# Routing weights of half the tokens: from one-hot matrix products to adding indirect DMAs and a GpSimd multiply

## The reference, cut to what matters

```
q = (ht @ w_q).reshape(T, PEER_HEADS, 2, PEER_HALF)
scores = einsum('thcd,hckd->thck', q, sub_keys)
s1, i1 = top_k(scores[:, :, 0], 16);  s2, i2 = top_k(scores[:, :, 1], 16)
cand_s = s1[..., :, None] + s2[..., None, :]          # 256 candidates a head
cand_i = i1[..., :, None] * 128 + i2[..., None, :]
top_s, pos = top_k(cand_s, 16);  idx = take_along_axis(cand_i, pos);  g = softmax(top_s)
act = gelu(einsum('pd,phkd->phk', hb, u[idx]))
out = einsum('phk,phkd->pd', g * act, v[idx])
```

## Time and profile before

| | |
|---|---|
| median of 3 runs | 2611.45 us |
| profiled execution, first to last instruction | 2611.0 us |
| busy PE, DVE, ACT, POOL | 2444.0, 1762.2, 1563.5, 28.8 us |
| mean granted clock of PE | 0.992 of full |
| moved by DMA | 413.64 MB, 158 GB/s |

### The profile page before, as it was taken

The page is one execution under the profiler, slowest core; times in us unless marked ns, Lnnn a source line. Parts: engine busy times, 40 slices in busy tenths (PEclk is TensorE's granted clock), DMA queues, the critical chain, the costliest instruction groups (busy, mean ns, idle before and its releaser), DMA issues.

```text
span 2611.0 us, 54286 instructions
## 1 busy us (share of the span) xinstructions
PE 2444.0 (94%) x16994; PEld 2251.7 (86%) x16994; DVE 1762.2 (67%) x4132; ACT 1563.5 (60%) x3546; POOL 28.8 (1%) x96
## 2 busy tenths in 40 slices
PE   8898989999999679999999989999999996899998
PEld 7798888999999568888899978899999995688887
DVE  4557775687774986666656667647777659766666
ACT  4476755555554875555556677456555558655555
POOL 0000100000000000000000001000000000000000
PEclk9999999999999999999999999999999999999999
DMA  5454445455555005555544543454555540255554
GB/s 186 168 174 137 146 146 176 148 187 181 178 176 181 12 33 194 192 192 194 192 168 163 171 132 121 162 177 161 178 187 181 177 145 0 81 193 193 193 193 169
DMA packets 116277, 413.64 MB, mean 158 GB/s; under 512 B 7860, under 2 KB 18028, under 8 KB 115948
## 3 DMA queue, kind: packets, MB, share of 16 engines
q1 hardware_dynamic: 116204, 412.73, 46.6%
HBM read 411.09 MB, written 4.23 MB: 159 GB/s over the span
## 4 chain that ended last, share of the span: by engine, by line
PE 80%; DVE 10%; ACT 4%; issue 3%; DMA 2%; DVEq 1%; ACTq 0%; POOL 0%; SPq 0%; POOLq 0%
PE bank L281 16%; PE bank L282 16%; PE bank L283 16%; PE bank L296 9%; PE bank L298 9%; PE bank L297 9%; DVE hot L1403 3%; DMA raw<-stream 2%; DVE w_lo L263 2%; DVE hot L1407 1%; ACT w_hi L250 1%; DVE A L1413 1%; PE bank L373 1%; ACT L323 1%; PE bank L1031 1%
## 5 line engine op out<-in xcount | busy, mean ns | idle before, releaser
L263 DVE TENSOR_TENSOR w_lo<-raw,w_hi 128x512 fp32r<-128x512 f32 x1512 | 1026.9, 689 | 772.1 <-ACT w_hi L250 761.0
L250 ACT ACTIVATE w_hi<-raw 128x512 fp32r<-128x512 f32 x1512 | 904.6, 626 | 390.2 <-PE bank L298 313.3
L281 PE MATMUL bank<-h_hi,w_hi 128*128 128x256 f32 x3488 | 999.5, 287 | 28.9 <-DVE w_lo L263 27.4
L282 PE MATMUL bank<-h_lo,w_hi 128*128 128x256 f32 x3488 | 989.0, 284 | 0.0
L283 PE MATMUL bank<-h_hi,w_lo 128*128 128x256 f32 x3488 | 988.7, 283 | 0.0
L281 PEld LDWEIGHTS bank<-h_hi,w_hi 128*128 128x128 f32 x3488 | 671.1, 192 | 39.9 <-DVE w_lo L263 31.8
L282 PEld LDWEIGHTS bank<-h_lo,w_hi 128*128 128x128 f32 x3488 | 671.3, 192 | 0.4
L283 PEld LDWEIGHTS bank<-h_hi,w_lo 128*128 128x128 f32 x3488 | 671.2, 192 | 0.0
L296 PE MATMUL bank<-w_hi,a_hi 128*128 128x512 f32 x1088 | 426.6, 392 | 8.3 <-issue 5.0
L297 PE MATMUL bank<-w_lo,a_hi 128*128 128x512 f32 x1088 | 425.9, 391 | 0.0
L298 PE MATMUL bank<-w_hi,a_lo 128*128 128x512 f32 x1088 | 425.3, 391 | 0.0
(11 more groups left out here) (180 smaller groups left out, 1881.8 us busy)
## 6 DMA issues: line engine op xcount, KB each, us to landing
raw<-stream SPq DMA_DIRECT2D x378, 1024.0 KB, 4.8
hank<-rel_hankel SPq DMA_DIRECT2D x16, 256.0 KB, 2.7
rel_hankel<-rel_line SPq DMA_DIRECT2D x8, 384.0 KB
hank<-rel_hankel SPq DMA_DIRECT2D x16, 128.0 KB, 2.2
A<-subkeys SPq DMA_DIRECT2D x2, 1024.0 KB, 4.9
x<-x_in SPq DMA_DIRECT2D x2, 512.0 KB, 3.8
pr<-lru_w SPq DMA_DIRECT2D x2, 512.0 KB, 7.3
out<-x SPq DMA_DIRECT2D x4, 256.0 KB, 2.0
```

The costliest lines, as they stand in the source:

```text
L250: act.activation(w_hi[:, (ring % 2) * 2 + k, :], raw[:, slot, sub, 512 * k:512 * k + 512], ACT.Copy).then_inc(w_hi_done, 1)
L263: dve.tensor_tensor(w_lo[:, q, :], raw[:, slot, sub, 512 * k:512 * k + 512], w_hi[:, q, :].bitcast(F32), ALU.subtract).then_inc(w_parts, 1)
L281: pe.matmul(ps, hi, rhs_hi(4 * k + c), start=first, stop=False)
L282: pe.matmul(ps, hi, rhs_lo(4 * k + c), start=False, stop=False)
```

## The change

Tokens 0 to 127 and tokens 128 to 255 are now treated apart.

- The top-k work is done in two passes over U, each for one half of the tokens (8 heads) and over 56 blocks (`HALF`): lists, candidates, candidate lists, softmax. The transposes stand behind block 116 (`FREE`) instead of 112.
- For tokens 0 to 127, DVE computes after the first pass, around block 53 of U, the address of each pick in a DRAM table `spread_w` (`cell_at` = index x 128 + token), and the weights `mass`. POOL then issues 128 indirect DMAs a layer, one for each head and rank, each of 128 single floats (one a partition, that is a token) that are added to the table in DRAM. Before the first of each head after the first it waits until all those of the heads before have landed.
- The tables (one a layer, 128 x 128 x 128 floats, 8 MB) are cleared by 16 DMAs a layer that POOL issues in the mixer, ahead of its wait for `on_sum`.
- When U is done, POOL fetches the table in 16 parts of 512 KB into four tiles that lie over `h_hi` and `h_lo`, and multiplies each into `A[:, 8i:8i+8, 0:128]`. The first split of V waits for the last of these too.
- The one-hot stage goes over tokens 128 to 255 alone: 32 groups instead of 64.

```diff
-N_GROUPS = SEQ // 4
+N_GROUPS = P // 4
@@ mix_gpsimd, between the last bias tile and the wait for on_sum
+                if layer == 0:
+                    pool.memset(zeros[:], 0.0).then_inc(zeros_set, 1)
+                    pool.wait_ge(zeros_set, 1)
+                for i in range(16):
+                    pool.dma_start(spread_w[layer][8 * i:8 * i + 8].rearrange("e (a b) t -> (e a) (b t)", a=16).rearrange("p (n f) -> p n f", f=512),
+                                   spread(zeros[:].rearrange("p (n f) -> p n f", n=1), 1, 2)).then_inc(cleared.sem, 16)
@@ the retrieval
-            FREE = 112
+            FREE = 116
+            HALF = 56
-            UNITS = TT * PEER_HEADS
+            UNITS = PEER_HEADS
+            def peer_gpsimd(pool, layer):
+
+                cells = spread_w[layer].rearrange("a b (t o) -> (a b t) o", o=1)
+                pool.wait_ge(cleared.sem, cleared.base)
+                pool.wait_ge(mass_done.sem, mass_done.base + 1)
+                for h in range(PEER_HEADS):
+                    if h:
+                        pool.wait_ge(scattered.sem, scattered.base + 16 * TOPK * h)
+                    for r in range(TOPK):
+                        pool.indirect_dma_start(cells, bass.IndirectOffsetOnAxis(ap=cell_at[:, h, r:r + 1], axis=0), mass[:, h, r:r + 1], None,
+                                                compute_op=ALU.add).then_inc(scattered.sem, 16)
+                pool.wait_ge(scattered.sem, scattered.base + 16 * P)
+                pool.wait_ge(up_read.sem, up_read.base + 2 + B_V)
+
+                def fetch(i):
+                    pool.dma_start(spread_tile[i % 4], spread_w[layer][:, 8 * i:8 * i + 8, :]).then_inc(spread_in[i % 4].sem, 16)
+                for i in range(4):
+                    fetch(i)
+                for i in range(16):
+                    pool.wait_ge(spread_in[i % 4].sem, spread_in[i % 4].base + 16 * (i // 4 + 1))
+                    part_a = A[:, 8 * i:8 * i + 8, 0:P]
+                    pool.tensor_tensor(part_a, part_a, spread_tile[i % 4], ALU.mult).then_inc(spread_done.sem, 1)
+                    if i + 4 < 16:
+                        pool.wait_ge(spread_done.sem, spread_done.base + i + 1)
+                        fetch(i + 4)
...
@@ DVE, after the first pass
+                soft_sum = soft_terms(0)
+                half(1)
+                dve.tensor_scalar(cell_at[:], sel_i, float(P), consts[:, C_ROW:C_ROW + 1], ALU.mult, ALU.add)
+                half(2)
+                half(3)
+                soft_weights(0, soft_sum, mass[:]).then_inc(mass_done.sem, 1)
...
@@ ACT, at block 53 of each pass
+                    act.wait_ge(soft_in.sem, soft_in.base + hf + 1)
+                    act.activation(sel_s, sel_s, ACT.Exp).then_inc(soft_out.sem, 1)
+                    table_of(act, ch, ACT.Gelu_apprx_tanh)
...
+                act.wait_ge(spread_done.sem, spread_done.base + 16)
                 act.wait_ge(g_read.sem, g_read.base + N_GROUPS)
                 part_hi(act, src, 0, 0)
...
@@ weigh
-                    a = A[:, :, bass.ds(g * 4, 4)]
+                    a = A[:, :, bass.ds(g * 4 + P, 4)]
```

More of the change, by code:

```diff
@@ L181, in trunk @@
         hankel = nc.dram_tensor("rel_hankel", (N_BIAS, P, SEQ), F32, kind="Internal").ap()
+        spread_w = [nc.dram_tensor(f"spread_w{l}", (P, KEYS, P), F32, kind="Internal").ap() for l in range(DEPTH)]
         raw_in = [sem(f"raw_in{i}") for i in range(2)]
@@ L1113, in trunk @@
             best_f = sb(part, "best_f", [P, TOPK])
-            whole = sb(part, "whole", [P, TT, P], I32)
+            whole = sb(part, "whole", [P, P], I32)
             diag_peer = picks[:, 0, :, :]
@@ L1212, in peer_scalar @@
[L1212 to L1229, removed]
@@ L1284, in peer_vector @@
                 blocks_loop(dve, 1, N_WQ - 1, ahead)
[L1287 to L1313, removed]
@@ L1315, in peer_vector @@
                 s_pair = s16.rearrange("p (u c) k -> p u c k", c=2)
                 i_pair = i16.rearrange("p (u c) k -> p u c k", c=2)
[L1317 to L1328, removed]
-                    ins = dve.scalar_tensor_tensor(out=cand_i[:, :, o:o + m], in0=i1, scalar=float(KEYS), in1=i2, op0=ALU.mult, op1=ALU.add)
-                    if i == PAIR_RANKS:
-                        ins.then_inc(cand_done.sem, 1)
-                    elif i < 7:
-                        split_half(dve, B_U + 33 + (i + 1) // 2, (1 + (i + 1) // 2) % 4, (i + 1) % 2)
@@ L1366, in peer_vector, with candidates @@
-                dve.drain()
-                half = lambda j: split_half(dve, B_U + 101 + j // 2, (1 + j // 2) % 4, j % 2)
+                def candidates(hf):
+                    at = B_U + HALF * hf + 17
+                    split_half(dve, at, 1, 0)
+                    dve.wait_ge(lists_out.sem, lists_out.base + 2 * hf + 2)
+                    for i in range(PAIR_RANKS + 1):
+                        m = CAND_N[i] if i < PAIR_RANKS else TOPK - PAIR_RANKS
+                        o = CAND_OFF[i]
+                        if i < PAIR_RANKS:
+                            s1, s2 = spread(s_pair[:, :, 0, i:i + 1], 2, m), s_pair[:, :, 1, 0:m]
+                            i1, i2 = spread(i_pair[:, :, 0, i:i + 1], 2, m), i_pair[:, :, 1, 0:m]
+                        else:
+                            s1, s2 = s_pair[:, :, 0, i:TOPK], spread(s_pair[:, :, 1, 0:1], 2, m)
+                            i1, i2 = i_pair[:, :, 0, i:TOPK], spread(i_pair[:, :, 1, 0:1], 2, m)
+                        dve.tensor_tensor(cand[:, :, o:o + m], s1, s2, ALU.add)
+                        ins = dve.scalar_tensor_tensor(out=cand_i[:, :, o:o + m], in0=i1, scalar=float(KEYS), in1=i2, op0=ALU.mult, op1=ALU.add)
+                        if i == PAIR_RANKS:
+                            ins.then_inc(cand_done.sem, 1)
+                        elif i < 7:
+                            split_half(dve, at + (i + 1) // 2, (1 + (i + 1) // 2) % 4, (i + 1) % 2)
@@ new lines, in soft_weights @@
+                def soft_weights(hf, soft_sum, out_w):
+                    dve.wait_ge(soft_out.sem, soft_out.base + hf + 1)
+                    ch(dve.tensor_reduce(soft_sum, sel_s, AX, ALU.add))
+                    ch(dve.reciprocal(soft_sum, soft_sum))
+                    return dve.tensor_tensor(out_w, sel_s, spread(soft_sum.rearrange("p (u o) -> p u o", o=1), 2, TOPK), ALU.mult)
+                best_lists(0)
+                candidates(0)
+                best_candidates(0)
+                half = lambda j: split_half(dve, B_U + 53 + j // 2, (1 + j // 2) % 4, j % 2)
@@ new lines, in peer_vector @@
+                half(2)
+                half(3)
+                soft_weights(0, soft_sum, mass[:]).then_inc(mass_done.sem, 1)
+                for j in range(4, 8):
+                    half(j)
+                best_lists(1)
+                candidates(1)
+                best_candidates(1)
+                half = lambda j: split_half(dve, B_U + 109 + j // 2, (1 + j // 2) % 4, j % 2)
+                half(0)
+                soft_sum = soft_terms(1)
+                half(1)
+                sel_i2 = sel_i.rearrange("p h k -> p (h k)")
@@ L1382, in peer_vector @@
                 half(3)
[L1383 to L1388 removed]
+                soft_weights(1, soft_sum, picks[:, 2, 1, :].rearrange("p (h k) -> p h k", h=PEER_HEADS)).then_inc(routed.sem, 1)
@@ L1389, in peer_vector @@
+                for j in range(4, 16):
                     half(j)
@@ L1451, in peer_tensor @@
                 for i in range(3):
[L1452 to L1454 removed]
+                    pe.transpose(bank[4 + i][:, 0:P], picks[:, i, 1, :], ident).then_inc(rt_done.sem, 1)
                 blocks_loop(pe, B_U + FREE, N_U - FREE, body)
@@ L1491, in _ @@
                     norm_pool(pool)
+                    peer_gpsimd(pool, layer)
                 begin(DEPTH, False)
```

212 lines of the change are left out of this document (131 added, 81 removed).

## The result

The changed kernel takes 2642.11 us (median of 4 runs, 2639.76 to 2646.11) against 2611.57 us before (4 runs): 1.0113 times as long, 95% interval 1.0101 to 1.0125. It was forecast at 2533 us, faster. Its profiled execution has a span of 2638.0 us, 27.0 more than before.

A forecast was written before the change was run, and what follows sets the result against it. PE bounds U and V, DVE the one-hot stage. Per layer 113.7 - 70 - 2.6 - 2.0 = 39.1 us gained, 78 for both: 2611 - 78 = 2533 us; own range 2505 to 2550, whole range 2500 to 2690.

The forecast's parts named there:

- step 4: POOL's indirect DMAs during U: 195 us a layer within 215 us, hidden with 20 us to spare.
- 128 x 1.4: Issue term of the scatter in POOL's queue: 128 indirect DMAs a layer at 1.4 us each.
- rival A: POOL's queue before the first fetch: scatter not over when U ends, up to 2682 us; chance 0.28 (c above 1.9).
- c = 1.93: Issue cost in us of an indirect DMA on POOL from which lateness, 48 us, makes the kernel slower.
- A's formula: Scatter lateness after U of 128 c + 16 - 215 us a layer, c being the issue cost; stage is lateness + 61.4.
- c = 1.75: Partly late scatter after U: 25 us late, 2561 us; 0.24 for the 2550 to 2590 range, shared with rival B.
- step 2: POOL's fetches and multiplies between U and V: 61.4 us a layer; 28 by the low ends, 85 by the high.
- step 3: One-hot stage, DVE's groups beside POOL's tail: 70 us a layer, 61.4 if undisturbed.
- rival B: One-hot stage: DVE and POOL exclude each other, stage 85 us, kernel 2563 us; chance 0.24, shared with partly late scatter.
- step 1: DVE's one-hot stage: 32 of 64 groups go, leaving 58.8 us a layer for DVE alone at 1.71 a group.
- steps 5, 6: Second softmax in U costs 2.6 us a layer; table clears in the mixer, with their 8 MB pass, 2 us.
- Rival C: U: POOL's descriptor work or added packets slow it by 77 us a layer, 2687 us; chance 0.08.

The follow-up runs named there:

- experiment 1: Changed kernel with only ranks 0 to 7 of each head scattered, 64 indirect DMAs a layer instead of 128: 2587.05 us.
- experiment 2: Changed kernel with each of the 128 indirect DMAs a layer over 64 addresses (partitions 0 to 63) instead of 128: 2586.62 us.
- experiment 4: Changed kernel, complete, with softmax and addresses of heads 0 to 2 at block 33 of U and heads 3 to 7 at block 57: 2591.98 us.
- experiment 9: Kernel of experiment 5 with the tensor_scalar one-hots reading the compared numbers from SBUF again: 2566.91 us.
- experiment 10: Kernel of experiment 5 with the tensor_tensor one-hot reading the compared numbers from SBUF again: 2572.65 us.
- experiment 8: Changed kernel with the numbers that the one-hots compare against read from PSUM, nothing else changed: 2632.41 us.
- experiment 5: Kernel of experiment 4 with the numbers that the one-hots compare against copied to PSUM once a layer and read there: 2530.71 us.

## Why the prediction was wrong

**Scatter (step 4): the step that failed.** The weights were ready when it said (637 us; the first indirect DMA starts at 637.87) and the last transfer lands at 921 to 923. The term "128 x 1.4" was mis-sized: an issue is 1.55 us at its shortest, 1.68 on the mean (429.6 us for 256), and 0.30 us of POOL's queue lie between two, which the sum did not have at all. Of the 90 us that 285 is more than the forecast 195, the dearer issues are 36, the gaps 49 and the waits 6. In all the scatter takes 922.9 - 637.9 = 285 us: 215 of issues, 49 of gaps (98.4 for both layers; 13 of them a layer above the regular 0.30, gaps of up to 4.1 us), and 22 of waits for landing, where I had 16. I had taken a value near the middle between SP's 0.37 us and a small transfer's 2.2 us, and the reason that I gave, an address for each partition, explains little of it: 64 addresses fewer save 0.14 us, the adding costs 0.60. With 285 us for 215 the scatter is 70 us late: rival A, for which I had c = 1.93 as the turning point. Issue and gap are 1.98 with the regular gap and 2.06 with all of them, and A's formula gives 128 x 2.06 + 16 - 215 = 65 us and 2611 + 2 x (65 + 66.0 - 113.7) = 2646 us; 2642 were measured. (The prediction's 2561 us for c = 1.75 does not follow from this formula, which gives 2566. It enters neither the forecast nor the range.)

**Tail (step 2): right within 8 us.** The multiply takes 2.35 us (2.2 taken), a fetch's issue 0.58 where 1.4 was taken. From 922.9 to 976.0 it is 53 us instead of 61.4. (The tail by the low ends is 29.2 us by the prediction's own terms, not 28; nothing rests on it.) The price in the Trainium skill, "GPSIMD Engine Reference", section 3.1, from which I had estimated 2.25 us, agrees with the trace within 5%.

**The two together (step 3): wrong, though hidden in the changed kernel.** There DVE had ended before POOL's first product, so it cost nothing; but the forecast of a hidden scatter rested on 70 us. It is 96 to 97 (experiments 1, 2 and 4), beyond the 85 of rival B. What failed was the reading of the earlier trace rows: that L900 and L263 ran unhindered beside a power of 16 elements in 3.28 us did not carry over to a multiply of 1024 elements in 2.35 us. And I let only L1403 be shut out, though L1407 is as well. The Trainium skill, "SBUF — State Buffer", section "Who interferes with whom", has both: a DVE instruction with two SBUF inputs contends with a GpSimd one that reads SBUF, and so does tensor_scalar in a two-port mode. Experiments 9 and 10 agree with each half (2.10 and 2.15 us beside POOL, 0.68 and 0.60 alone), and in experiment 1 DVE comes free as POOL's instruction ends. Why the power does not hold DVE is not shown. With the scatter in time the forecast of 2533 us, and its own range up to 2550, would have been missed all the same: 2587 us is what such a kernel takes.

**Groups (step 1)** held: 32 at 1.71 us. **Softmax and clears (steps 5, 6):** together the stage starts 2.6 us later in layer 0 and another 4.0 in layer 1; 4.6 a layer were taken. Both lie within the spread of such starts: experiments 1, 2 and 8, which differ from the changed kernel ahead of the stage only in the indirect DMAs (1, 2) or by one short copy (8), start it at 851.3, 855.8 and 856.5 us. PE's stop at the added softmax is 2.1 us, the 16 clears were issued in 11.64 us where 21.2 were free, and DVE's L966 starts at 341.9 against 341.66.

**Rival C** did not come true in the changed kernel: PE is busy for 212.67 of 215 us of U beside the scatter.

## What to carry to other kernels

Work that is moved to an idle engine has to be priced there by the instruction and its gap, and multiplied out, before its overlap is counted: 0.66 us too little on an issue with its gap was 84 us when there were 128. Before two engines are set side by side, go through each instruction form for the port that both use; here one operand in PSUM instead of SBUF, at 0.12 us a group, was worth 61 us in the kernel of experiment 5. A chain in the background whose steps can't be made cheaper can still be started earlier, piece by piece, as soon as its first input is there (experiment 4: 60 us).

## What the runs showed of the hardware

- An adding indirect DMA of 128 single floats takes POOL 1.55 us at the shortest and 0.30 us up to the next; without the addition 0.96 us, with 64 addresses 1.41 us (medians; 1.56 for the first). It is 144 packets, and 32 without the addition. A plain fetch of 512 KB is issued in 0.58 us and lands in 3.8 us.
- A POOL product of 128 x 1024 floats takes 2.35 us and is not slowed by DVE; DVE's tensor_tensor on two SBUF operands and its tensor_scalar from SBUF to SBUF wait until it ends (3.22 and 3.10 us, experiment 1), those with an operand in PSUM don't (0.71 and 0.75 us, experiment 5). Four products without a fetch between them held one pair for 9.98 us.
- With 128 plain indirect DMAs a layer of single floats PE was busy for 49 of 163 us of U, the stream fell from 180 to 33 GB/s, and the kernel took 2899 us; the adding ones left U as it was. The cause is open.
